# The last output chunk of five projections computed and added in two halves of 256 tokens

## The chip, the cores and the metric

The kernel runs on one core of a Trainium2 chip. The metric is the device time of one execution in microseconds (us); lower is better. Of the kernel before, three runs took 3549.62, 3550.29 and 3558.47 us, median 3550.29 us. A core has five engines that run side by side and meet at semaphores: TensorE (PE: matmuls; PEld: its weight loads), VectorE (DVE), ScalarE (ACT), GpSimd (POOL) and SyncE (SP), which issues the DMAs. Matmuls write to eight PSUM banks, each of 512 f32 columns on 128 partitions.

## The reference

A sequence of 512 tokens of width 1024 goes through two blocks. The first has two layers, each a gated feed-forward, a mixer (a recurrent hybrid in the first layer, an mLSTM in the second) and another gated feed-forward, and a final norm; the second block has attention, an RWKV mixer and a feed-forward. What the change touches are the last steps of four feed-forwards and of the mLSTM, where the output of a projection is scaled and added to the residual `x`:

```python
h = modulate(x, 0)
x = x + HALF_STEP * (1.0 + mod[:, 0, 2]) * swiglu(h, ffn_w_gate[layer, 0], ffn_w_up[layer, 0], ffn_w_down[layer, 0])
h = modulate(x, 1)
...
x = x + (1.0 + mod[:, 1, 2]) * y.astype(x.dtype)

def swiglu(h, w_gate, w_up, w_down):
    return (jax.nn.silu(h @ w_gate) * (h @ w_up)) @ w_down

def modulate(t, sub):
    return rms_norm(t, norm_g[layer, sub]) * (1.0 + mod[:, sub, 1]) + mod[:, sub, 0]
```

The mean of the squares of `x` in `rms_norm` goes over the 1024 channels of each token, so the norm behind a projection needs all of its output chunks.

## The kernel before

Activations lie with channels on the 128 partitions and the 512 tokens along the free dimension: the residual `K.x` is eight chunks (DC = 8) of 128 channels by 512 tokens. To keep f32 accuracy, weights and activations are each split into a rounded part in fp32r (`hi`) and the rest (`lo`), and each product is three matmuls: `w_hi`*`hi`, `w_hi`*`lo`, `w_lo`*`hi`.

`gemm` runs all large products. It takes the weights in tiles, four to a turn. SP loads a tile into `w_raw` (ring of four), ScalarE writes `w_hi` (`split_hi`, L253), VectorE writes `w_lo` (`split_lo`, L259), each into one of two halves of its buffer (by the tile's number, even or odd), and TensorE multiplies (L464 to L466), three matmuls for each block of 128 inputs. Behind a tile's last matmul `tile_mm` counts up. The turns run as a loop in each engine's own program, the last turn apart in straight code (`last` is true). Each engine works its program strictly in the order in which it is written; nothing but the semaphores ties them.

`project` calls `gemm` for the down projections of the four gated feed-forwards (called by `swiglu`, activations `f_gu_hi`, `f_gu_lo`, 22 input blocks) and for that of the mLSTM (`ml_hi`, `ml_lo`, 16 blocks). Two weight tiles make one output chunk (`tpo` = 2), of 11 or 8 input blocks each, accumulated in one bank: tiles j = 0, 1 of a turn in bank 0, tiles j = 2, 3 in bank 1. So a chunk is 66 matmuls of 512 columns, 48 in the mLSTM. Behind the second tile VectorE updates the residual, `x = bank * coef + x` (L1261), and counts `bank_free` up. That releases ScalarE: the square of the new chunk (L614, tiles `sq_f`, `sq_ml`; at the last feed-forward a second, scaled square, L616), then `h_hi` = `gain` * `x` (`ahead_act`, L723). GpSimd sums the squares of the first seven chunks; VectorE writes `h_lo` (`ahead_dve`, L728).

Behind each of these projections stands a gemm whose input norm is begun early (`follow`, a `Modulated`): its first tile (`early_tile`, L419 to L423) multiplies the weights with `gain` * `x` before the norm is known, chunk by chunk. Between its matmuls TensorE adds up the squares (`between`, L746) and, once VectorE has the reciprocal root, spreads it into a row (L121). The result of the early tile is scaled afterwards. The second and third tile (`next_pair`, L435, L436, banks 1 and 2) use the normed input.

Of the kernel before, what the change touches and what calls it, by code (L numbers as in the profile page):

```python
# [16 lines left out]
ALU = mybir.AluOpType  # L17
# [4 lines left out]
S = 512  # L22
NT = S // P
D = 1024
DC = D // P
FF = 2816
FC = FF // P
RING = 4
# [118 lines left out]
def setup(nc, ctx, dram):  # L147
    K = Core()
# [51 lines left out]
    K.hi_done = K.count("w_hi_done")  # L200
    K.lo_done = K.count("w_lo_done")
    K.tile_mm = K.count("tile_mm")
    K.bank_free = K.count("bank_free")

    K.ada_loaded, K.ada_base = [K.sem(f"ada_loaded{i}") for i in range(2)], 0
# [74 lines left out]
    body(n - 1, True)  # L280


def gemm(K, w, kb, n_tiles, nxt, mm, pe_wait, act_evac=None, dve_evac=None, turn=4, post=None, side=None, head=None, squares=None, fetched=RING, fetch=RING, aside=None, slots_free=None, dve_first=None, unroll=False, pe_more=None, pool_work=None, sp_more=None, dve_lead=None, ready_k=None, begun=False):

    nc = K.nc
# [5 lines left out]
    with one_block(K) as block:  # L293
# [90 lines left out]
        def _(pe):  # L384
# [3 lines left out]
            def weights(j, k):  # L388
                return K.w_hi[:, j % SPLIT, k * P:(k + 1) * P], K.w_lo[:, j % SPLIT, k * P:(k + 1) * P]

            def first_pair():
                for j in range(2):
                    pe.wait_ge(K.lo_done.sem, g0 + j + PRIMED + 1)
                    pe_wait(pe, 0, j, j)
                for k in range(kb):
                    pe.wait_ge(K.h_hi_done.sem, K.h_hi_done(k + 1))
                    for j in range(2):
                        hi, lo, bank, start, stop = mm(k, j)
                        wh, wl = weights(j, k)
                        nc.tensor.matmul(K.ps[bank][:], wh, hi, start=start, stop=False)  # L400
                        nc.tensor.matmul(K.ps[bank][:], wl, hi, start=False, stop=False)  # L401
                for j in range(2):
                    for k in range(kb):
                        hi, lo, bank, start, stop = mm(k, j)
                        pe.wait_ge(K.h_ready.sem, K.h_ready(k + 1))
                        last_mm = nc.tensor.matmul(K.ps[bank][:], weights(j, k)[0], lo, start=False, stop=stop)  # L406
                    last_mm.then_inc(K.tile_mm.sem, 1)
# [37 lines left out]
            def body(i, last):  # L445
                for j in range(turn):
                    t = turn * i + j
                    if early and isinstance(i, int) and t < 3:
                        if t == 0:
                            early_tile()  # L450
                        if t == 1:
                            next_pair()
                    elif head and isinstance(i, int) and t < 2:
                        if t == 0:
                            first_pair()
                    elif not (begun and t == 0):
                        pe.wait_ge(K.lo_done.sem, g0 + t + PRIMED + 1)
                        pe_wait(pe, i, j, t)
                        for k in range(kb):
                            if ready_k and isinstance(i, int) and t == 0:  # L460
                                ready_k(pe, k)
                            hi, lo, bank, start, stop = mm(k, j)
                            wh, wl = weights(j, k)
                            nc.tensor.matmul(K.ps[bank][:], wh, hi, start=start, stop=False)  # L464
                            nc.tensor.matmul(K.ps[bank][:], wh, lo, start=False, stop=False)  # L465
                            last_mm = nc.tensor.matmul(K.ps[bank][:], wl, hi, start=False, stop=stop)  # L466
                        last_mm.then_inc(K.tile_mm.sem, 1)
                    if pe_more:
                        pe_more(pe, t)
                    if side and last and j == turn - 1:  # L470
                        side.reduce(pe, n)
# [715 lines left out]
def swiglu(K, name, w_gu, w_down, nxt, head, gate, ada=None, double=False, follow=None):  # L1187
# [27 lines left out]
    def dve_evac(dve, i, j, t, mm_done):  # L1215
        f = 2 * i + j // 2
        if j % 2 == 1:
# [5 lines left out]
                                    gu_hi[:, bass.ds(f, 1), :].bitcast(F32), ALU.subtract).then_inc(K.gu_lo_done.sem, 1)  # L1223

    gemm(K, w_gu, DC, 2 * FC, (w_down, KB_MAX), mm, pe_wait, act_evac, dve_evac, side=side, head=head)
    low = K.gu_lo_done(0)
    for c in (done, sil_done, guhi_done, K.gu_lo_done):
# [12 lines left out]
def root_table(K, act):  # L1240

    K.nc.scalar.activation(K.pad4[:], K.consts[:, 0:NT], ACT.Sqrt)


def project(K, w, kb, tpo, mm, nxt, gate, half, squares, turn=4, side=None, ready=None, follow=None):

    nc = K.nc
    banks = turn // tpo
    free = K.bank_free

    def pe_wait(pe, i, j, t):
        if j % tpo == 0:
            pe.wait_ge(free.sem, free(banks * i + j // tpo - banks + 1))
        if ready:
            ready(pe, j)

    def dve_evac(dve, i, j, t, mm_done):
        if j % tpo == tpo - 1:
            o = banks * i + j // tpo
            dve.wait_ge(K.tile_mm.sem, mm_done)  # L1260
            nc.vector.scalar_tensor_tensor(K.x[:, bass.ds(o, 1), :], K.ps[j // tpo][:, None, :], K.coef[:, bass.ds(o, 1)], K.x[:, bass.ds(o, 1), :],  # L1261
                                           ALU.mult, ALU.add).then_inc(free.sem, 1)
            if follow:
                follow.ahead_dve(dve, o)

    def act_evac(act, i, j, t, mm_done):
        if j % tpo == tpo - 1:
            o = banks * i + j // tpo
            if isinstance(o, int) and o == DC - 1:
                root_table(K, act)  # L1270
            act.wait_ge(free.sem, free(o + 1))
            if follow:
                act.wait_ge(K.x_written.sem, K.x_written(follow.GAIN_STEPS))
            squares.by_act(act, K.x[:, bass.ds(o, 1), :], o, j // tpo % 2)
            if follow:
                follow.ahead_act(act, o)

    def coefficients(dve):
        dve.wait_ge(free.sem, free(0))
        dve.wait_ge(K.ada_out.sem, K.ada_out(0))  # L1280
        nc.vector.tensor_scalar(K.coef[:], gate, 1.0, half, ALU.add, ALU.mult).then_inc(K.coef_done.sem, 1)
        dve.wait_ge(K.coef_done.sem, K.coef_done(1))
        if follow:
            follow.gain_ahead(dve)

    gemm(K, w, kb, DC * tpo, nxt, mm, pe_wait, act_evac, dve_evac, turn=turn, side=side, squares=squares, dve_first=coefficients)
    if follow:
        follow.ahead_advance()
    free.base += DC
    K.coef_done.base += 1  # L1290
# [2427 lines left out]
def build(nc, dram, plan=None):  # L3718
    with ExitStack() as ctx:
        K = setup(nc, ctx, dram)  # L3720
        K.prod_done = K.count("prod_done")
        K.conv_step = K.count("conv_step")
# [159 lines left out]
```

## Time and profile before

| | us |
|---|---|
| median of three runs | 3550.29 |
| span of the profiled execution, first to last instruction | 3552.7 |
| time of the profiled execution around its span | not recorded apart |
| TensorE busy | 3415.0 (96%) |
| VectorE busy | 2019.4 (57%) |
| ScalarE busy | 1212.5 (34%) |
| mean granted TensorE clock | 0.982 of 2.4 GHz |

An engine that is busy for nearly all of the span sets the time wherever it has no gap. A matmul's time in the rows runs from its start to the arrival of its result, and the next starts before that; how long a stream of matmuls takes is read from the starts. The start times in the rows are us from the span's start.

### The profile page before, as it was taken

The page shows a single profiled execution, that of the slowest core. Times are in us where ns is not written, and L with a number is a line of the kernel's source. Part 1 is how long each engine was busy: PE and PEld are TensorE (multiplying, and loading weights), DVE is VectorE, ACT ScalarE, POOL GpSimd, SP SyncE. Part 2 cuts the span into 40 slices and gives each one's busy share as a digit, 9 for nine tenths or more (in the row PEclk, how much of TensorE's full clock was granted, in tenths as well). Part 3 has the DMA queues.
Part 4 walks back from the last instruction along what each step waited for, and adds up shares of the span by engine and source line. Part 5 has one row for each costly group of instructions (what it writes and reads, how often), then busy time and mean ns, then how long its engine had stood idle before and what let it go on. Part 6 is the DMA issues. An engine that isn't in the chain of part 4 may idle for free. (4 is left out here: it accounts for less than half of the span.)

```text
span 3552.7 us, 56318 instructions
## 1 busy us (share of the span) xinstructions
PE 3415.0 (96%) x22324; PEld 2767.9 (78%) x22324; DVE 2019.4 (57%) x2820; ACT 1212.5 (34%) x1783; POOL 361.9 (10%) x264
## 2 busy tenths in 40 slices
PE   7999998999999999999999999999989999999998
PEld 5888777778888788876678888877767787878886
DVE  6666666856665766574443433365666773454343
ACT  3222346432222322243243322233434543233231
POOL 1000003410000000010101000130103330010000
PEclk9999999999999999999999999999979999989999
DMA  6554322125554555421032233232210002223332
GB/s 246 194 195 174 129 74 72 56 93 189 194 204 140 183 189 205 162 87 48 1 107 94 95 97 103 90 90 82 62 37 6 7 7 68 95 66 101 95 95 77
DMA packets 103764, 382.73 MB, mean 108 GB/s; under 512 B 11424, under 2 KB 15136, under 8 KB 103200
## 3 DMA queue, kind: packets, MB, share of 16 engines
q1 hardware_dynamic: 103584, 380.15, 31.8%
q8 instruction: 135, 2.21, 0.3%
q14 instruction: 45, 0.37, 0.0%
HBM read 378.01 MB, written 2.10 MB: 107 GB/s over the span
## 5 line engine op out<-in xcount | busy, mean ns | idle before, releaser
L464 PE MATMUL bank<-h_hi,w_hi 128*128 128x512 f32 x2576 | 1015.5, 394 | 30.1 <-DVE w_lo L259 27.3
L466 PE MATMUL bank<-h_hi,w_lo 128*128 128x512 f32 x2576 | 1005.3, 390 | 0.0
L465 PE MATMUL bank<-h_lo,w_hi 128*128 128x512 f32 x2576 | 1005.1, 390 | 0.0
L259 DVE TENSOR_TENSOR w_lo<-w_raw,w_hi 128x1024 fp32r<-128x1024 f32 (+2 forms) x480 | 635.2, 1323 | 386.5 <-ACT w_hi L253 375.4
L253 ACT ACTIVATE w_hi<-w_raw 128x1024 fp32r<-128x1024 f32 (+2 forms) x475 | 521.3, 1097 | 287.7 <-PE bank L466 247.9
L464 PEld LDWEIGHTS bank<-h_hi,w_hi 128*128 128x128 f32 x2576 | 485.2, 188 | 147.2 <-DVE w_lo L259 30.7
L466 PEld LDWEIGHTS bank<-h_hi,w_lo 128*128 128x128 f32 x2576 | 485.1, 188 | 102.7
L465 PEld LDWEIGHTS bank<-h_lo,w_hi 128*128 128x128 f32 x2576 | 485.3, 188 | 100.5 <-issue 1.9
L464 PE MATMUL bank<-f_gu_hi,w_hi 128*128 128x512 f32 x704 | 274.2, 390 | 0.0
L466 PE MATMUL bank<-f_gu_hi,w_lo 128*128 128x512 f32 x704 | 273.9, 389 | 0.0
L465 PE MATMUL bank<-f_gu_lo,w_hi 128*128 128x512 f32 x704 | 273.9, 389 | 0.0
L1213 ACT ACTIVATE f_gu_hi<-f_prod_t 128x512 f32 (+1 forms) x88 | 55.6, 632 | 406.9 <-DVE f_prod_t L1220 406.9
L558 DVE SCALAR_TENSOR_TENSOR ada_acc<-ada_tiles,c_act,ada_acc 128x512 f32<-128x512 f32 x210 | 157.4, 750 | 6.9 <-DMA ada_tiles<-in_ada 1.2
L1220 DVE TENSOR_TENSOR f_prod_t<-f_sil_t,bank 128x512 f32<-128x512 f32 x88 | 60.5, 687 | 166.8 <-PE bank L466 166.8
L466 PEld LDWEIGHTS bank<-f_gu_hi,w_lo 128*128 128x128 f32 x704 | 132.1, 188 | 27.6
L464 PEld LDWEIGHTS bank<-f_gu_hi,w_hi 128*128 128x128 f32 x704 | 132.1, 188 | 27.6
L465 PEld LDWEIGHTS bank<-f_gu_lo,w_hi 128*128 128x128 f32 x704 | 132.1, 188 | 27.4
L1210 ACT ACTIVATE f_sil_t<-bank 128x512 f32<-128x512 f32 x88 | 52.7, 598 | 243.8 <-PE bank L466 243.7
L1261 DVE SCALAR_TENSOR_TENSOR residual<-bank,coef,residual 128x512 f32 (+1 forms) x40 | 30.0, 751 | 156.9 <-PE bank L466 156.9
L607 POOL MEMSET sq_acc_f<- 128x512 f32 x5 | 2.6, 528 | 1039.5 <-DVE f_gu_lo L1222 1039.5
L1222 DVE TENSOR_TENSOR f_gu_lo<-f_prod_t,f_gu_hi 128x512 f32 (+1 forms) x88 | 60.9, 692 | 77.9 <-ACT f_gu_hi L1213 77.9
L466 PE MATMUL bank<-u_hi,w_lo 128*128 128x512 f32 x256 | 99.6, 389 | 0.0
(643 smaller groups left out, 4730.2 us busy)
## 6 DMA issues: line engine op xcount, KB each, us to landing
ada_tiles<-in_ada SPq DMA_DIRECT2D x180, 512.0 KB, 4.1
w_raw<-in_gu SPq DMA_DIRECT2D x176, 512.0 KB, 4.4
w_raw<-in_dn SPq DMA_DIRECT2D x64, 704.0 KB, 4.8
w_raw<-in_w_ff SPq DMA_DIRECT2D x64, 512.0 KB, 3.6
w_raw<-in_w_hyb SPq DMA_DIRECT2D x36, 512.0 KB, 3.3
w_raw<-in_w_rkv SPq DMA_DIRECT2D x24, 512.0 KB, 3.6
w_raw<-in_w_attn SPq DMA_DIRECT2D x20, 512.0 KB, 3.6
w_raw<-in_w_hout SPq DMA_DIRECT2D x16, 512.0 KB, 3.4
```

The costliest lines, as they stand in the source:

```text
L253: K.nc.scalar.activation(K.w_hi[:, half, 0:kb * P], K.w_raw[:, slot, 0:kb * P], ACT.Copy).then_inc(K.hi_done.sem, 1)
L259: K.nc.vector.tensor_tensor(K.w_lo[:, half, 0:kb * P], K.w_raw[:, slot, 0:kb * P], K.w_hi[:, half, 0:kb * P].bitcast(F32), ALU.subtract).t ...
L464: nc.tensor.matmul(K.ps[bank][:], wh, hi, start=start, stop=False)
L465: nc.tensor.matmul(K.ps[bank][:], wh, lo, start=False, stop=False)
L466: last_mm = nc.tensor.matmul(K.ps[bank][:], wl, hi, start=False, stop=stop)
L558: ins = v.scalar_tensor_tensor(self.acc[:], block, c, self.acc[:], ALU.mult, ALU.add)
L607: self.K.nc.gpsimd.memset(acc[:], 0.0).then_inc(self.K.sq_added.sem, 1)
L1210: nc.scalar.activation(sil[:, j // 2, :], K.ps[j][:], ACT.Silu).then_inc(sil_done.sem, 1)
L1213: nc.scalar.activation(gu_hi[:, bass.ds(f, 1), :], prod[:, j // 2:j // 2 + 1, :], ACT.Copy).then_inc(guhi_done.sem, 1)
L1220: nc.vector.tensor_tensor(prod[:, j // 2, :], sil[:, j // 2, :], K.ps[j][:], ALU.mult).then_inc(done.sem, 1)
L1222: nc.vector.tensor_tensor(gu_lo[:, bass.ds(f, 1), :], prod[:, j // 2:j // 2 + 1, :], gu_hi[:, bass.ds(f, 1), :].bitcast(F32), ALU.subtract ...
L1261: nc.vector.scalar_tensor_tensor(K.x[:, bass.ds(o, 1), :], K.ps[j // tpo][:, None, :], K.coef[:, bass.ds(o, 1)], K.x[:, bass.ds(o, 1), :], ...
```

## The change

In the last turn, the last two weight tiles (j = 2 and 3, the last output chunk) are no longer multiplied with all 512 tokens at a time. `tile_in_halves` runs over the tile's input blocks for tokens 0 to 255 into columns 0 to 255 of bank 1, then again for tokens 256 to 511 into columns 256 to 511 of bank 2. Behind the last matmul of the first half of tile 3 a new semaphore, `half_mm`, counts up. VectorE updates the residual in two instructions of 256 columns: the first waits for `half_mm`, the second for `tile_mm` as before, and it alone counts `bank_free` up. ScalarE's work on the chunk, and `h_lo`, stay whole.

```diff
@@ gemm, TensorE
+            def tile_in_halves(j):
+                for part in range(2):
+                    cols = slice(part * (S // 2), (part + 1) * (S // 2))
+                    for k in range(kb):
+                        hi, lo, bank, start, stop = mm(k, j)
+                        wh, wl = weights(j, k)
+                        out = K.ps[bank + part][:, cols]
+                        nc.tensor.matmul(out, wh, hi[:, cols], start=start, stop=False)
+                        nc.tensor.matmul(out, wh, lo[:, cols], start=False, stop=False)
+                        last_mm = nc.tensor.matmul(out, wl, hi[:, cols], start=False, stop=stop)
+                    if part == 0 and j == turn - 1:
+                        last_mm.then_inc(K.half_mm.sem, 1)
+                return last_mm
...
-                        for k in range(kb):
+                        in_halves = last_in_halves and last and j >= turn - 2
+                        if in_halves:
+                            last_mm = tile_in_halves(j)
+                        for k in range(0 if in_halves else kb):
@@ project, VectorE
+    def half_evac(o, part):
+        cols = slice(part * (S // 2), (part + 1) * (S // 2))
+        x = K.x[:, o, cols]
+        return nc.vector.scalar_tensor_tensor(x, K.ps[(turn - 1) // tpo + part][:, cols], K.coef[:, o:o + 1], x, ALU.mult, ALU.add)
...
+            if isinstance(o, int) and o == DC - 1:
+                dve.wait_ge(K.half_mm.sem, K.half_mm(1))
+                half_evac(o, 0)
+                dve.wait_ge(K.tile_mm.sem, mm_done)
+                half_evac(o, 1).then_inc(free.sem, 1)
+                if follow:
+                    follow.ahead_dve(dve, o)
+                return
...
-    gemm(K, w, kb, DC * tpo, nxt, mm, pe_wait, act_evac, dve_evac, turn=turn, side=side, squares=squares, dve_first=coefficients)
+    gemm(K, w, kb, DC * tpo, nxt, mm, pe_wait, act_evac, dve_evac, turn=turn, side=side, squares=squares, dve_first=coefficients, last_in_halves=True)
+    K.half_mm.base += 1
```

TensorE's program before, where the last tile (j = 3) of the first feed-forward's down projection begins. Names: `w_hi`, `w_lo` are the split weights, `f_gu_hi`, `f_gu_lo` the split activations.

```order
L464 MATMUL bank<-f_gu_hi,w_hi 128x512
L465 MATMUL bank<-f_gu_lo,w_hi 128x512
L466 MATMUL bank<-f_gu_hi,w_lo 128x512
L464 MATMUL bank<-f_gu_hi,w_hi 128x512 [waits gu_lo_done,w_lo_done]
L465 MATMUL bank<-f_gu_lo,w_hi 128x512
L466 MATMUL bank<-f_gu_hi,w_lo 128x512
```

The same place in TensorE's program after the change.

```order
L399 MATMUL bank<-f_gu_hi,w_hi 128x256
L400 MATMUL bank<-f_gu_lo,w_hi 128x256
L401 MATMUL bank<-f_gu_hi,w_lo 128x256
L399 MATMUL bank<-f_gu_hi,w_hi 128x256 [waits gu_lo_done,w_lo_done]
L400 MATMUL bank<-f_gu_lo,w_hi 128x256
L401 MATMUL bank<-f_gu_hi,w_lo 128x256
```

The three matmuls of a block are half as wide, and from the wait to the end of the tile there are 66 of them instead of 33. The waits stay where they were; in all, TensorE's program grows by 312 matmuls in the five projections.

VectorE's program before, at the end of the same projection and the start of the next gemm. `ada_acc`, `ada_turned`, `ada_parts` and `mods` belong to modulation weights worked on in between.

```order
L259 TENSOR_TENSOR w_lo<-w_raw,w_hi 128x1024 [waits w_hi_done]
L564 STREAM_TRANSPOSE ada_turned_212<-ada_acc_211 128x512 [waits ada_step]
L566 TENSOR_REDUCE ada_parts_213<-ada_turned_212 128x16 [waits ada_turned]
L1261 SCALAR_TENSOR_TENSOR residual<-bank,coef,residual 128x512 [waits tile_mm]
L728 SCALAR_TENSOR_TENSOR h_lo<-residual,gain,h_hi 128x512 [waits h_hi_done]
L573 TENSOR_TENSOR mods<-bank,cols 128x16 [waits ada_mm]
```

The same place in VectorE's program after the change.

```order
L260 TENSOR_TENSOR w_lo<-w_raw,w_hi 128x1024 [waits w_hi_done]
L582 STREAM_TRANSPOSE ada_turned_212<-ada_acc_211 128x512 [waits ada_step]
L584 TENSOR_REDUCE ada_parts_213<-ada_turned_212 128x16 [waits ada_turned]
L1278 SCALAR_TENSOR_TENSOR residual<-bank,coef,residual 128x256 [waits half_mm]
L1278 SCALAR_TENSOR_TENSOR residual<-bank,coef,residual 128x256 [waits tile_mm]
L746 SCALAR_TENSOR_TENSOR h_lo<-residual,gain,h_hi 128x512 [waits h_hi_done]
L591 TENSOR_TENSOR mods<-bank,cols 128x16 [waits ada_mm]
```

One update became two, the first with a wait of its own; nothing else changed its place.

## Rows read from the trace of the kernel before

**Rows 1.** Page, engines' busy time; two costly groups: count, busy, mean ns, idle before.

```profile
PE 3415.0 (96%) x22324; PEld 2767.9 (78%) x22324; DVE 2019.4 (57%) x2820; ACT 1212.5 (34%) x1783; POOL 361.9 (10%) x264
...
L1220 DVE TENSOR_TENSOR f_prod_t<-f_sil_t,bank 128x512 f32<-128x512 f32 x88 | 60.5, 687 | 166.8 <-PE bank L466 166.8
...
L1261 DVE SCALAR_TENSOR_TENSOR residual<-bank,coef,residual 128x512 f32 (+1 forms) x40 | 30.0, 751 | 156.9 <-PE bank L466 156.9
```

**Rows 2.** Busy time by stretch: stretch, length, PE, PEld, DVE, ACT, POOL, clock, DMA.

```profile
393.00:408.00 15.00, 15.00 (x71) 12.15 (x69) 8.92 (x10) 5.07 (x6) 1.29 (x1) 1.00 0.11 36
...
1941.00:1952.00 11.00, 11.00 (x50) 9.09 (x49) 4.38 (x4) 4.74 (x6) 1.29 (x1) 1.00 0.16 51
```

**Rows 3.** Time order, first feed-forward's end: start us, us, instruction [idle before].

```profile
393.13 0.75 DVE L1261 SCALAR_TENSOR_TENSOR residual<-bank,coef,residual 128x512 f32<-128x512 f32 x1 [4.38 <-PE bank L466]
...
403.64 0.69 DVE L566 TENSOR_REDUCE ada_parts<-ada_turned 128x16 f32<-128x512 f32 x1
...
408.09 0.75 DVE L1261 SCALAR_TENSOR_TENSOR residual<-bank,coef,residual 128x512 f32<-128x512 f32 x1 [3.76 <-PE bank L466]
...
408.87 0.63 ACT L614 ACTIVATE sq_f<-residual 128x512 f32<-128x512 f32 x1 [5.63 <-DVE residual L1261]
...
409.41 0.71 ACT L723 ACTIVATE h_hi<-residual,gain 128x512 fp32r<-128x512 f32 x1
...
410.15 0.75 DVE L728 SCALAR_TENSOR_TENSOR h_lo<-residual,gain,h_hi 128x512 fp32r<-128x512 f32 x1 [1.31 <-ACT h_hi L723]
...
410.55 0.42 PEld L746 LDWEIGHTS bank<-consts,sq_f 128*128 128x128 f32 x2
```

**Rows 4.** Time order, the mLSTM projection's last two chunks and its end.

```profile
1941.23 0.75 DVE L1261 SCALAR_TENSOR_TENSOR residual<-bank,coef,residual 128x512 f32<-128x512 f32 x1 [3.06 <-PE bank L466]
...
1952.11 0.75 DVE L1261 SCALAR_TENSOR_TENSOR residual<-bank,coef,residual 128x512 f32<-128x512 f32 x1 [3.06 <-PE bank L466]
...
1952.90 0.63 ACT L614 ACTIVATE sq_ml<-residual 128x512 f32<-128x512 f32 x1 [3.59 <-DVE residual L1261]
...
1954.17 0.42 PEld L746 LDWEIGHTS bank<-consts,sq_ml 128*128 128x128 f32 x2
```

**Rows 5.** Time order, the early tile's first matmul on its last chunk.

```profile
416.39 0.47 PE L419 MATMUL bank<-h_hi,w_hi 128*128 128x512 f32 x1
```

**Rows 6.** Time order, the last update of the third feed-forward.

```profile
1523.93 0.75 DVE L1261 SCALAR_TENSOR_TENSOR residual<-bank,coef,residual 128x512 f32<-128x512 f32 x1 [3.76 <-PE bank L466]
```

**Rows 7.** Time order, the last feed-forward's end: second square, first read of squares.

```profile
2318.31 0.71 ACT L616 ACTIVATE sq_f<-residual,cols 128x512 f32<-128x512 f32 x1
...
2320.87 0.28 PE L746 MATMUL bank<-consts,sq_f 128*128 128x1 f32 x2
```

**Rows 8.** Weight loads of 16 and 128 columns; time order, matmuls with 16-column loads.

```profile
L1471 PEld LDWEIGHTS bank<-h_hi,w_dt_hi x8: 94/94/95, 459.9 to 464.8; 128*16 128x16 f32 x8
...
L464 PEld LDWEIGHTS bank<-f_gu_hi,w_hi 128*128 128x128 f32 x704 | 132.1, 188 | 27.6
...
460.16 0.40 PE L1471 MATMUL bank<-h_hi,w_dt_hi 128*16 128x512 f32 x1
...
465.44 0.39 PE L1471 MATMUL bank<-h_hi,w_dt_lo 128*16 128x512 f32 x1
```

**Rows 9.** Time order, mLSTM scores in f32: 512-column matmuls; loads at 256, 128.

```profile
1643.28 2.74 PE L2137 MATMUL bank<-ml_xc,ml_y 128*128 128x512 f32 x6
...
1651.04 1.70 PEld L2137 LDWEIGHTS bank<-ml_xc,ml_y 128*128 128x128 f32 x8
...
1652.77 0.86 PEld L2137 LDWEIGHTS bank<-ml_xc,ml_y 128*128 128x128 f32 x7
```

**Rows 10.** Time order, two of the early tile's matmuls, a pair of L746 between.

```profile
410.47 0.47 PE L419 MATMUL bank<-h_hi,w_hi 128*128 128x512 f32 x1
...
410.92 0.48 PE L421 MATMUL bank<-h_lo,w_hi 128*128 128x512 f32 x1
```

**Rows 11.** Groups by line and shape, a VectorE read of 256 bank columns.

```profile
L2330 DVE TENSOR_TENSOR mlh_e<-mlh_e,bank 128x256 f32<-128x256 f32 x4 | 1.7, 419 | 0.0
```

More of the change, by code:

```diff
@@ L202, in setup @@
     K.tile_mm = K.count("tile_mm")
+    K.half_mm = K.count("half_mm")
     K.bank_free = K.count("bank_free")
@@ L280, in rolled, with gemm @@
     body(n - 1, True)
-def gemm(K, w, kb, n_tiles, nxt, mm, pe_wait, act_evac=None, dve_evac=None, turn=4, post=None, side=None, head=None, squares=None, fetched=RING, fetch=RING, aside=None, slots_free=None, dve_first=None, unroll=False, pe_more=None, pool_work=None, sp_more=None, dve_lead=None, ready_k=None, begun=False):
+def gemm(K, w, kb, n_tiles, nxt, mm, pe_wait, act_evac=None, dve_evac=None, turn=4, post=None, side=None, head=None, squares=None, fetched=RING, fetch=RING, aside=None, slots_free=None, dve_first=None, unroll=False, pe_more=None, pool_work=None, sp_more=None, dve_lead=None, ready_k=None, begun=False, last_in_halves=False):
     nc = K.nc
```

## The prediction, made before the changed kernel ran

> **What bounds the kernel now.** I read the page's busy times first: TensorE is busy for 96% of the span, VectorE for 57%, and only TensorE is near to being full [rows 1]. The change touches five places, the last of eight output chunks of each of the five projections that call `project` (the four down projections of the gated feed-forwards, tile names `f_gu`, and that of the mLSTM, `ml`). So the second view is the busy time by stretch there: in the last chunks TensorE is busy for the whole stretch, at a granted clock of 1.00, that is 2.4 GHz [rows 2]. A stage without a gap on TensorE gets longer by whatever TensorE gets to do, and shorter only if the wait behind it gets shorter.
>
> The third view is the order in time around the first of these ends. A chunk of 66 matmuls of 128x512 takes 408.09 - 393.13 = 14.96 us, which is 226.7 ns per matmul [rows 3]. The mLSTM's chunk of 48 takes 1952.11 - 1941.23 = 10.88 us, again 226.7 ns [rows 4].
>
> What waits for the last residual update? It starts at 408.09 and takes 0.75 us; ScalarE then squares it (to 409.50) and writes `h_hi` (to 410.12), VectorE `h_lo` (to 410.90) [rows 3]. TensorE meanwhile has gone on with the next gemm's early tile, whose first columns read older chunks. It first needs the last square for the sum of squares, whose weight load starts at 410.55 [rows 3]: 1.05 us after the square was there. It needs `h_lo` of the last chunk only at 416.39 [rows 5], and the root, the row and the scaled input hang on TensorE's own sums. The two ends after it, of which one row stands [rows 6], repeat this pattern. At the mLSTM the square ends at 1953.53 and its load starts at 1954.17, 0.64 us later [rows 4]; at the last feed-forward the second square ends at 2319.02 and is read at 2320.87 [rows 7]. So at none of the five ends does TensorE wait for the update.
>
> **The change part by part.**
>
> TensorE's work. The last two weight tiles of each projection go from 33 (mLSTM: 24) matmuls of 512 columns each to twice as many of 256, each with its own weight load. That is 4 x 66 + 48 = 312 matmuls replaced by 624, in both tiles, not only in the one whose end is waited for. They take 312 x 0.2267 = 70.7 us now. The new time is 624 x p, where p is the spacing of 256-column matmuls of this type with a 128x128 load each. The trace has none in fp32r, so I bound it:
>
> - From below by the load alone. A load of 16 columns takes 94 ns and one of 128 takes 188 [rows 8], so 0.839 ns a column, 107.4 ns for 128 columns. 624 x 0.1074 - 70.7 = -3.7 us.
> - The mLSTM's scores in plain f32 show the same situation: their 128-column records stream for as long as 256 columns do here (two clocks a column, since the 256-column ones come every (1.70 - 0.19)/7 = 0.216 us) and carry a full load, and they come every (0.86 - 0.19)/6 = 0.112 us [rows 9]. So loads of 188 ns are started every 112 ns, and load and stream overlap. p = 0.112: 69.9 - 70.7 = -0.8 us.
> - If the excess over pure streaming is a share of the columns, p = 226.7/2 = 113.4 ns and the change costs nothing.
> - If the excess is fixed per matmul: 512 columns at 2.4 GHz are 213.3 ns, so it is 13.4 ns; p = 106.7 + 13.4 = 120.1 ns, and the cost is 312 x 13.4 ns = 4.2 us.
> - If the load's spacing and the excess add: the early tile gives (0.45 - 0.227)/2 = 0.112 us for each of the two full loads with one column behind it that lie between two of its matmuls [rows 3, 10]; p = 112 + 13.4 = 125.4 ns, +7.5 us.
> - Farthest: a load must be over (188 ns) before the next matmul starts. 624 x 0.188 - 70.7 = +46.6 us.
>
> I take the fixed excess, 120 ns. Two rows speak for it. The spacing stays at (465.44 - 460.16)/23 = 0.230 us where the load has 16 columns instead of 128 [rows 8], so the excess isn't load time left uncovered. And in f32 the excess does not grow with the columns: (2.74 - 0.59)/5 = 0.43 us apart at 512 columns (426.7 ns of streaming, 3 over), 0.216 at 256 (213.3, again 2 to 3 over) [rows 9]. Result: +3.5 us at the feed-forwards, 264 x 13.4 ns, and +0.6 at the mLSTM, 48 x 13.4 ns.
>
> Here a page of the Trainium skill speaks against the change. "Perfetto Trace Analysis", section "Matmuls", says that larger matmuls are more efficient than smaller ones; "TensorE: Matmul & The Clock Gate", section "Back-to-back issue gap", puts a warm matmul at its columns over 2.4 GHz plus about 2.5 ns, that is 215.8 and 109.2 ns. By it, as an estimate, the change would cost 312 x 2.5 ns = 0.8 us. The trace has 226.7 ns for 512 columns of fp32r, so of its excess the page has a fifth, and the measurement decides.
>
> VectorE's work. One update of 751 ns from a bank becomes two of 256 columns. Reads of a bank with two operands take 687 ns at 512 columns [rows 1] and 419 at 256 [rows 11], 1.05 ns a column, so a half takes 751 - 268 = about 0.48 us. The first half's matmuls end some 33 x 0.12 = 4.0 us before the second's; its 0.48 us lies in the time in which VectorE waits anyway (3.76 us idle ahead of the update) [rows 3]. Only the second half is left behind the last matmul, and the update ends 0.27 us earlier. It is worth nothing, since TensorE needs what follows 0.64 us later than it has it, or more. Behind the new wait for `half_mm` stand on VectorE only the second half, `h_lo`, and `w_lo` of the next gemm; no one needs the latter two earlier than before. If both halves fell behind the last matmul, the update would end 2 x 0.48 - 0.75 = 0.21 us later, and that is covered too.
>
> ScalarE, GpSimd, SP. Their order doesn't change. They see the last two tiles end about 0.44 and 0.88 us later, while the next gemm's first tile is split into `w_hi` and `w_lo` and stored in a part of the buffer that the last tile doesn't read; that is done well inside the last tile's 7.9 us. No DMA is added. Bank 2, which now takes the second half, is next written by the pair of tiles behind the early tile, which come after the matmul at 416.39 [rows 5], 7 us behind the update. The new matmuls stand in straight code, so 312 more pairs of load and matmul are fetched; I cost that at nothing, since the f32 pairs of rows 9 came every 112 ns. If that cover were gone it would be a case of rival 1.
>
> **Sum.** +4.2 us of TensorE, 0 on the rest. The profiled execution's span is 3552.7 us, 2.4 us over the median of the runs, 3550.3, whose own scatter is 3549.6 to 3558.5. On the median: 3550.3 + 4.2 = 3554.5 us, or +0.12%. About 0.3%, 10.7 us, is what a measurement of this kernel can tell from no change, so this reads as the same.
>
> **Rivals.**
>
> 1. The load shows (slower). With half the columns to hide under, the fp32r load and its switch into the array aren't covered. For it: load and stream are now equally long, 107 ns each, where before the stream had twice the load's length; no row shows this pair in fp32r. Against it: f32 with the same two lengths comes at 112 ns [rows 9]. It decides from p = (70.7 + 10.7)/624 = 130.5 ns; at 125 ns the kernel still reads the same. At 188 ns: 3550.3 + 46.6 = 3596.9 us; at 140, 3566.9 us.
> 2. Smaller pieces cost nothing, and the earlier update counts (slightly faster, but within the 0.3%). p = 112 ns gives -0.8 us; if all five ends passed on the 0.27 us, -1.4 more: 3548.1 us. Against it: the slack of 0.64 us or more at each end. A gain of over 0.3% has no row: even p at the load's floor with all updates counted gives -5.1 us, 3545.2.
> 3. The change doesn't do what it says: the first half's update runs together with the second's, since VectorE is late or the semaphore comes late. VectorE's last piece of work ahead of it ends at 404.33 [rows 3], about when the first half is ready (408.09 - 4.0 = 404.1). It costs 0 as worked out, so the time is that of the forecast, 3554.5; only the trace would tell.
>
> **How the numbers follow.** Forecast (fixed excess, +1 to +8 us), with rival 3 in it: 0.70. Excess by share or less, rival 2: 0.15. Rival 1 beyond 130.5 ns: 0.12. A gain of over 0.3% by a mechanism that I don't see: 0.03. So faster 0.03, same 0.85, slower 0.12. The likeliest one's own range is 3551.3 to 3558.3. The range goes from rival 2 with a microsecond of scatter, 3547, to above the sum of load spacing and excess (3557.8) with the runs' scatter, 3561; about 0.08 of rival 1 is left out above, some 0.05 below.
>
> **What would show it.** In the groups by line the matmuls of 256 columns should be 1.1 to 1.25 us per ten apart, and each last chunk of a feed-forward 15.8 us long instead of 14.96, the mLSTM's 11.5 instead of 10.88. The first half's update should stand about 4 us before the second's, each near 0.48 us, and the square should start 0.27 us sooner after the last matmul, with TensorE's next wait unchanged. I am wrong if the last chunks are 14.9 us or shorter (then the excess goes by columns, rival 2), if they are over 17.2 us (rival 1), or if TensorE's sum of squares moves up against the end of the projection.

## The result and the profile after

Slower, by more than was forecast. Five runs of the changed kernel took 3561.44 to 3571.29 us, median 3565.12, beside 3551.0 us for the kernel before on the same chip: ratio 1.0038, 95% interval 1.0024 to 1.0052. The forecast was 3554.5 us and its range ended at 3561. So some 4 us were foreseen and some 9 to 10 were not. The profiled run is the slowest of the five; its page begins:

```profile
span 3569.5 us, 56947 instructions
...
PE 3426.7 (96%) x22636; PEld 2789.8 (78%) x22636; DVE 2021.1 (57%) x2825; ACT 1212.8 (34%) x1783; POOL 359.6 (10%) x264
```

TensorE has 22636 - 22324 = 312 matmuls more [rows 1] and the same share of a longer span. The stretches of the two kinds of last chunk, columns as in [rows 2]:

```profile
393.00:409.00 16.00, 16.00 (x139) 15.79 (x138) 9.48 (x12) 5.13 (x7) 1.29 (x1) 1.00 0.11 34
1942.00:1954.00 12.00, 12.00 (x95) 11.65 (x94) 4.87 (x5) 4.75 (x6) 1.29 (x1) 1.00 0.25 89
```

TensorE is still without a gap there, at 2.4 GHz, and its weight loads now fill 15.79 of 16 us where they filled 12.15 of 15 [rows 2]. The matmuls themselves in time order (start us, us, engine, line, operation):

```profile
394.54 0.28 PE L399 MATMUL bank<-f_gu_hi,w_hi 128*128 128x256 f32 x1
394.66 0.28 PE L400 MATMUL bank<-f_gu_lo,w_hi 128*128 128x256 f32 x1
394.78 0.28 PE L401 MATMUL bank<-f_gu_hi,w_lo 128*128 128x256 f32 x1
```

They start 0.12 us apart. The end of the first feed-forward, which answers to [rows 3], idle time before each in brackets:

```profile
392.59 0.75 DVE L1292 SCALAR_TENSOR_TENSOR residual<-bank,coef,residual 128x512 f32<-128x512 f32 x1 [4.38 <-PE bank L484]
...
404.46 0.48 DVE L1278 SCALAR_TENSOR_TENSOR residual<-bank,coef,residual 128x256 f32<-128x256 f32 x1 [0.24 <-PE bank L401]
...
408.42 0.48 DVE L1278 SCALAR_TENSOR_TENSOR residual<-bank,coef,residual 128x256 f32<-128x256 f32 x1 [3.47 <-PE bank L401]
408.94 0.63 ACT L632 ACTIVATE sq_f<-residual 128x512 f32<-128x512 f32 x1 [5.80 <-DVE residual L1278]
...
410.89 0.42 PEld L764 LDWEIGHTS bank<-consts,sq_f 128*128 128x128 f32 x2
```

The last chunk takes 408.42 - 392.59 = 15.83 us, 0.87 more than before. The first half is updated 3.96 us ahead of the second, and the square starts 0.52 us after the last update's start instead of 0.78 [rows 3]: 0.26 us earlier. TensorE loads that square at 410.89, 1.32 us after it was there. The mLSTM's end, which answers to [rows 4]:

```profile
1944.10 0.75 DVE L1292 SCALAR_TENSOR_TENSOR residual<-bank,coef,residual 128x512 f32<-128x512 f32 x1 [3.06 <-PE bank L484]
...
1955.61 0.48 DVE L1278 SCALAR_TENSOR_TENSOR residual<-bank,coef,residual 128x256 f32<-128x256 f32 x1 [2.40 <-PE bank L401]
```

11.51 us instead of 10.88. So all five places cost 4 x 0.87 + 0.63 = 4.1 us, as forecast. The rest is not at the places that were edited: at the last of them the last update starts 4.3 us later than before (2321.31 instead of 2316.99), at the start of the RWKV stage, which the change doesn't touch, the trace is 6 us behind, at that stage's end 11 and at the kernel's end 17. By stretch, the kernel before:

```profile
2695.00:2958.00 263.00, 245.34 (x7300) 211.23 (x7299) 182.04 (x399) 123.42 (x230) 89.93 (x59) 1.00 0.03 7
2958.00:2989.00 31.00, 25.02 (x169) 17.32 (x159) 15.09 (x24) 11.77 (x16) 0.00 (x0) 0.94 0.26 87
```

The changed one:

```profile
2701.00:2969.00 268.00, 246.81 (x7271) 211.85 (x7263) 182.17 (x399) 123.50 (x230) 89.39 (x59) 0.99 0.03 7
2969.00:3006.00 37.00, 29.05 (x184) 20.04 (x184) 15.09 (x24) 11.66 (x16) 0.00 (x0) 0.86 0.25 86
```

The same work has 268.0 - 246.8 = 21.2 us without a matmul instead of 17.7, and a stretch at 1.2 GHz follows behind it (granted clock 0.86 instead of 0.94 over a stretch 6 us longer).

### The profile page after: what moved, and what is told of

It reads as the page before. It is cut to its first block and busy times, and to the rows that moved or that the text cites. A ratio compares the mean times of both kernels' runs of the same rounds, so it can differ in the third digit from the quotient of the medians.

```text
span 3569.5 us, 56947 instructions
## 1 busy us (share of the span) xinstructions
PE 3426.7 (96%) x22636; PEld 2789.8 (78%) x22636; DVE 2021.1 (57%) x2825; ACT 1212.8 (34%) x1783; POOL 359.6 (10%) x264
## 5 line engine op out<-in xcount | busy, mean ns | idle before, releaser
L482 PE MATMUL bank<-f_gu_hi,w_hi 128*128 128x512 f32 x616 | 240.0, 390 | 0.0
L484 PE MATMUL bank<-f_gu_hi,w_lo 128*128 128x512 f32 x616 | 239.7, 389 | 0.0
L483 PE MATMUL bank<-f_gu_lo,w_hi 128*128 128x512 f32 x616 | 239.6, 389 | 0.0
L482 PEld LDWEIGHTS bank<-f_gu_hi,w_hi 128*128 128x128 f32 x616 | 115.6, 188 | 24.3
L484 PEld LDWEIGHTS bank<-f_gu_hi,w_lo 128*128 128x128 f32 x616 | 115.6, 188 | 24.0
L483 PEld LDWEIGHTS bank<-f_gu_lo,w_hi 128*128 128x128 f32 x616 | 115.7, 188 | 23.9
L482 PE MATMUL bank<-u_hi,w_hi 128*128 128x512 f32 x256 | 99.6, 389 | 0.0
```

## Where TensorE runs out of instructions

What ended the idle time ahead of TensorE's weight loads in that stage (us, times, longest), the kernel before:

```profile
PEld bank L3200 <- issue: 8.1, 19, 0.8
...
PEld bank L3320 <- issue: 2.4, 2, 1.3
```

The changed one; L3232 and L3352 are the same lines of the program:

```profile
PEld bank L3232 <- issue: 11.2, 23, 1.1
...
PEld bank L3352 <- issue: 2.1, 1, 2.1
```

"issue" means that nothing in the profile released the engine. The transfers show what some of it was. In the transfers of 8 us of the changed kernel (GB/s in 40 slices of 0.2 us) the only ones are of instructions:

```profile
GB/s 0 0 82 0 0 0 0 0 0 0 0 0 0 0 0 0 0 0 0 0 0 0 82 0 0 0 0 0 0 0 0 0 0 0 0 0 0 0 0 0
...
q8 instruction: 2, 0.03, 1.5%
```

They start at 2930.4 and 2934.5 us. TensorE's loads after a pause, same time:

```profile
2932.91 0.13 PEld L3333 LDWEIGHTS bank<-rw_rbkT,rw_W 64*64 64x64 f32 x1 [0.77 <-issue]
2936.94 0.13 PEld L3352 LDWEIGHTS bank<-rw_b_tok,rw_W 64*64 64x64 f32 x1 [2.07 <-issue]
```

Each instruction packet of this queue in the trace has 16384 bytes. The stage's 57 packets (this view, both kernels) stand against some 14,600 loads and matmuls (7300 and 7299 in the row of the kernel before above), which makes 256 instructions a packet. I counted TensorE's instructions through the trace: both of these pauses end at the same place modulo 256 (number 90 of the records), exactly 256 records apart, 1.4 and 1.6 us after a packet has landed. I take that place for the first instruction of a block. A pause is measured here from the start of the instruction before it, so it is some 0.1 us longer than the idle time in the rows. Taking all pauses of over 0.35 us at such a block start that end 1.2 to 1.7 us after a landing, the kernel before has 10, of 10.3 us together, all in the RWKV stage; the changed one 16, of 16.5 us. The other "issue" pauses of that length in the stage stand elsewhere in the blocks, and there are some 20 of them in either trace: those at block starts are what has grown, from 10 to 16. There the code is straight and pairs of load and matmul follow each other within some 20 ns where nothing is waited for, so a block is used up in 2 to 3 us, while the closest transfers of these traces start 3.3 us apart. Where a block holds a wait for VectorE or GpSimd, the next one arrives meanwhile. Where a whole block falls into fast code, TensorE pauses at both its ends, as at 2932.91 and 2936.94. In the kernel before the block starts fall elsewhere in the same code:

```profile
2925.28 0.13 PEld L3312 LDWEIGHTS bank<-rw_W,rw_b_tok 64*64 64x64 f32 x1 [0.89 <-issue]
2927.19 0.54 PEld L3200 LDWEIGHTS bank<-rw_abT_T,rw_off 64*64 64x64 f32 x16 [0.17 <-POOL rw_off L3103]
```

One pause of 0.89 us, none at L3320, and at 2927.19 TensorE waits for GpSimd as it should. In the changed kernel it comes late there instead.

The Trainium skill, "Runtime: NRT & Kernel Launch", section "Instruction fetch mechanics", describes this: instructions arrive in blocks of 16 KiB, 256 of them, the next one fetched while the present one runs. On the size the trace agrees. The page also holds that crossing a block is mostly hidden, and names taken branches as what makes an engine wait for its instructions; here code without a branch pauses 10 to 16 us. The experiments are to tell whether the pauses make the loss.

## The experiments

Each ratio stands against runs of the kernel before on the same chip; e13 ran once and has none. Each kernel's time is split in two parts: the mean over its runs of span x granted clock, and the rest, span x (1 - clock). The first is roughly the time if the clock had never fallen to 1.2 GHz, the second what the fallen clock took. A mean over 8 to 12 runs is good to about 1 us in either part, one over 5 to about 2. The kernel before has 3483.7 + 67.0 us over 99 runs on four chips, whose means at full clock agree within 0.4 us; the two columns are differences from it. "Pauses" are those at block starts, from one profile of each.

| kernel | median us | ratio and interval | at full clock | lost to clock | pauses, us |
|---|---|---|---|---|---|
| before | 3551 to 3553 | | 0 | 0 | 10, 10.3 |
| changed (both series, 10 runs) | 3565.12, 3567.04 | 1.0038 (1.0024 to 1.0052), 1.0037 (1.0024 to 1.0050) | +9.4 | +4.0 | 16, 16.5; 17, 16.1 |
| e1 more matmuls | 3555.99 | 1.001 (1.0001 to 1.0019) | +4.1 | -0.4 | 10, 8.5 |
| e2 624 waits | 3558.75 | 1.0016 (1.0007 to 1.0025) | +4.9 | +1.2 | 16, 14.6 |
| e3 changed + 656 waits | 3565.46 | 1.0029 (1.0019 to 1.0039) | +10.1 | +1.2 | 11, 10.4 |
| e4 changed + 400 waits | 3556.15 | 1.0013 (1.0004 to 1.0022) | +4.7 | +0.3 | 11, 9.5 |
| e5 changed, one update | 3565.6 | 1.0035 (1.0022 to 1.0049) | +9.3 | +2.9 | 17, 14.2 |
| e6 38 waits | 3552.6 | 0.9996 (0.9987 to 1.0005) | -0.3 | -0.5 | 14, 9.4 |
| e7 1024 waits | 3554.44 | 1.0 (0.9991 to 1.001) | 0.0 | +0.8 | 10, 9.0 |
| e8 112 waits | 3564.57 | 1.0027 (1.0018 to 1.0037) | +6.0 | +3.9 | 16, 14.1 |
| e9 192 waits | 3559.71 | 1.002 (1.0011 to 1.0028) | +5.6 | +1.5 | 14, 13.7 |
| e10 64 waits | 3552.53 | 1.0 (0.9991 to 1.0009) | +1.3 | -1.4 | 14, 10.2 |
| e11 112 waits, all at the last place | 3557.62 | 1.0015 (1.0005 to 1.0024) | +5.3 | -0.4 | 19, 16.9 |
| e12 changed + 144 waits | 3557.86 | 1.0017 (1.0008 to 1.0026) | +4.7 | +0.3 | 11, 10.7 |

**The changed kernel again**, unaltered.

> The changed kernel once more, unaltered. The first measurement gave +14 us (3565.1 against 3551.0), of which its trace shows only 4.3 us in the five last chunks (matmuls 120 ns apart as forecast, 0.93 us per feed-forward and 0.6 at the mLSTM); the rest lies elsewhere, most of it in the RWKV stage and beside stretches at the lower clock. Theory A (the rest is systematic and comes from TensorE's program being 624 instructions longer, which moves the code behind it): again +14 us, 3565. Theory B (the rest is chance of that set of runs, the lower-clock stretches falling differently): +4.3 us, 3555. Theory C (the rest is systematic and comes from the delay itself, which moves the later stages in time): again +14 us.

It repeats: 3567.04 us (3562.07 to 3568.26). Not chance.

**The matmuls' cost alone (e1), and the length of the code alone (e2).** e1 adds to the kernel before as much matmul time as the halves, 19 matmuls of 512 columns into the unused bank 2, hence 38 instructions:

```diff
+                            if extra and last and j >= turn - 2 and k == kb - 1:
+                                for _ in range(extra[j - turn + 2]):
+                                    nc.tensor.matmul(K.ps[2][:], wh, hi, start=True, stop=True)
```

> The kernel before, with the last chunk whole, but with 19 more matmuls of 512 columns into bank 2 (2 in each of the last two tiles of the four feed-forwards, 1 and 2 in those of the mLSTM): 19 x 0.2267 = 4.3 us more of TensorE at the same five places, and only 38 more instructions in its program. The results in bank 2 are not read. Theory A (code length): +4.3 us and little more, 3555. Theory B (chance): +4.3 us, 3555. Theory C (the delay has consequences): +14 us, 3565.

e2 adds as many instructions as the halves, 624, but waits that are satisfied already, up to two ahead of a matmul. Two calls of `wait_ge` in a row become one instruction, hence the `2 * n`: TensorE has 1161 semaphore instructions in e2's trace and 537 in that of the kernel before.

```diff
+            def fill(wanted):
+                n = min(pad[0], left[0]) if wanted else 0
+                left[0] -= n
+                for _ in range(2 * n):
+                    pe.wait_ge(K.lo_done.sem, g0 + PRIMED)
...
+                            fill(pad and last and j >= turn - 2)
                             nc.tensor.matmul(K.ps[bank][:], wh, hi, start=start, stop=False)
```

> The kernel before, with the last chunk whole, but with two more semaphore instructions (waits that are long satisfied) ahead of each matmul of the last two tiles, 624 in all: TensorE's program is as much longer as in the changed kernel, at the same five places, with no work added to the array. The waits should be hidden while the matmuls are 226.7 ns apart. Theory A (code length): about +10 us, 3561. Theory B (chance) and theory C (delay): 0, 3551. If the waits aren't hidden, the last chunks get longer, and their length in the trace says by how much.

e1 costs 4.1 us at full clock and moves nothing else: a delay of this size is passed on once and starts nothing. e2 does no work and costs 4.9 us at full clock (its expectation had about 10 us in all by the length of the code; 6.1 were found in the mean span). Its matmuls still come every 0.22 to 0.23 us:

```profile
1943.78 0.39 PE L473 MATMUL bank<-ml_hi,w_hi 128*128 128x512 f32 x1
1944.00 0.39 PE L475 MATMUL bank<-ml_lo,w_hi 128*128 128x512 f32 x1
1944.23 0.39 PE L477 MATMUL bank<-ml_hi,w_lo 128*128 128x512 f32 x1
```

So its loss isn't where the waits are. The place of the code behind them is left.

**The changed kernel with its code moved on to a multiple of 256 (e3, e4, e12).** The waits of e2 in the first two tiles of the last turn (`j < turn - 2`): e3 fills up each of the five places to 256 instructions, e4 leaves out the mLSTM and reaches 1024 in all, e12 reaches 768.

> The changed kernel, with satisfied waits between the 512-column matmuls of the two tiles ahead of the halves (124 per feed-forward, 160 in the mLSTM), so that each of the five places adds 256 instructions to TensorE's program instead of 132 or 96. If the rest of the loss is the position of the later code relative to blocks of a power of two up to 256 instructions (theory A in its narrow form), it goes: +4.3 us, 3555. If it is the mere amount of code (A in its wide form), it doubles or so: +14 to +25 us. Theory B: +4.3 us. Theory C: +14 us.

> The changed kernel, with satisfied waits between 512-column matmuls ahead of the halves, at most two per matmul (in e3 four per matmul set the spacing at 0.44 us in the mLSTM's projection and cost some 7 us; two were hidden): 124 in each of the first three feed-forwards, 28 in the last, none in the mLSTM. TensorE's program is 1024 instructions longer than before the change when the RWKV stage begins, 4 x 256. Theory A (the position of the later code relative to blocks of 256 instructions; pauses of TensorE without a releaser stand at instructions 89 to 92 modulo 256 in all traces so far): the RWKV stage from 2695 to 2957 us is as long as before the change, within 0.5 us, and the kernel costs +4.3 us for the matmuls and up to 2 for the stretch at 549 us: 3556 to 3558. Theory A' (amount of code): +14 us or more, 3566.

> The changed kernel with 36 satisfied waits in the first two tiles of the last turn of each of the four feed-forwards, 144 in all: with the 624 instructions that the halves add this is 768, three blocks of 256. Place theory: only the cost of the matmuls is left, +4.3 us over the kernel before (+3 to +7), and the RWKV stage has 10 to 11 pauses at block starts of 9 to 10.5 us together. Rival (the recovery with 1024 had to do with where those waits stood or with chance): +11 to +14 us as in the changed kernel, and about 16 pauses of 14 to 16.5 us.

e3 gave nothing back in all, for a reason of its own: four waits ahead of each of the mLSTM's matmuls are too many.

```profile
1943.84 0.47 PE L491 MATMUL bank<-ml_hi,w_hi 128*128 128x512 f32 x1
1944.28 0.47 PE L493 MATMUL bank<-ml_lo,w_hi 128*128 128x512 f32 x1
1944.72 0.47 PE L495 MATMUL bank<-ml_hi,w_lo 128*128 128x512 f32 x1
```

At 0.44 us each they made that stage 6 to 7 us longer, which hid the recovery; the pauses were back at 11, of 10.4 us. e4 and e12, without that, both fall to 4.7 us over the kernel before at full clock, which is the matmuls' cost, and lose nothing to the clock. In e4 the RWKV stage answers to the kernel before (262.0 - 244.7 = 17.3 us without a matmul, 17.7 there):

```profile
2697.00:2959.00 262.00, 244.74 (x7250) 210.56 (x7243) 181.62 (x399) 123.49 (x230) 89.97 (x59) 1.00 0.03 7
2959.00:2991.00 32.00, 26.04 (x211) 18.32 (x203) 15.44 (x26) 11.78 (x16) 0.00 (x0) 0.95 0.26 88
```

and its idle time ahead of the same line is again what it was, to the tenth:

```profile
PEld bank L3243 <- issue: 8.1, 19, 0.8
```

More instructions made the changed kernel 8.3 us faster in the mean span (3564.0 to 3555.7). The waits replaced nothing, so what they did was to move the later code. The stretch at the lower clock near 549 us, of which the expectations of e4 and e5 speak, isn't a mark of the halves: between 545 and 556 us the granted clock is 1.00 in e4 and e12, which hold them, and 0.84 in e9, which doesn't.

**One update again (e5).** The matmuls stay in halves, both into bank 1, `half_mm` goes, and VectorE updates all 512 tokens behind the last:

```diff
-                        out = K.ps[bank + part][:, cols]
+                        out = K.ps[bank][:, cols]
...
-            if isinstance(o, int) and o == DC - 1:
+            if False:
```

> The changed kernel with the halves of the matmuls kept, but both into bank 1, without the semaphore for the first half, and with the residual updated whole in one instruction behind the last matmul. If the early half of the update is worth nothing (the forecast): the same time as the changed kernel, 3566, within 2 us. If it is worth the 0.27 us at each of the five ends: 1.4 us more, 3567. If part of the loss (the extra stretch at the lower clock near 549 us, seen in three of three traces with halves and in none of the others) comes from VectorE's two updates: 1 to 3 us less, 3563.

3565.6 us, as with two updates. The earlier update gains nothing that can be measured.

**Moving the code of the kernel before (e6 to e11).** The waits of e2, of other numbers: 38, 1024, 112 (624 less twice 256), 192 and 64, spread over the feed-forwards, and in e11 all 112 at the last of the places.

> The kernel before, with 38 satisfied waits in the last two tiles of the five projections (8 in each feed-forward, 6 in the mLSTM) and no other work: the later code of TensorE stands where it stands in e1. There the RWKV stage from 2695 to 2957 us was 2.9 us shorter than before the change. Theory A: the same here, -2 to -3 us in that stage, 3549 to 3551 in all. Theory A' (amount of code) and chance: 0 in that stage, within 0.5 us.

> The kernel before, with 256 satisfied waits in the last turn of each of the four feed-forward projections (two per matmul), 1024 in all, and no other work. Theory A: the later code keeps its place relative to blocks of 256, so the RWKV stage is as long as before within 0.5 us and the time is 3552 within 1.5 us. Theory A' (amount of code): 1024 instructions cost more than the 624 of e2, which cost 5.7 us: +9 us, 3561.

> The kernel before, with 112 satisfied waits (28 in each feed-forward projection) and no other work. 112 is what 624, the lengthening by the change, leaves over 512. Theory A (place relative to blocks of 256 instructions): the RWKV stage from 2695 to 2957 us is as long as with the change and in e2, 266 to 268 us instead of 262.4, and the time is +4 to +6 us, 3557 to 3559. Theory A'' (any lengthening that isn't a multiple costs in proportion to its amount): 112/624 of e2's loss, +1 us, 3554, and 263.4 us in the stage.

> The kernel before, with 192 satisfied waits (48 in each feed-forward projection). A scan for the place of the later code at which the pauses cost least. Theory A says only that the stage's length will lie in the band seen so far, 259 to 268 us, and be set by the place; theory A'' says +1.8 us in the stage, 264.2.

> The kernel before, with 64 satisfied waits (16 in each feed-forward projection). As e9: at 38 the stage took 259.4 and 260.9 us, at 112 it should take 266 to 268, so theory A says 260 to 268 here; theory A'' says +0.6 us, 263.0.

> The kernel before with 112 satisfied waits of TensorE (no array work), all in the last two tiles of the fourth feed-forward, the last of the five places ahead of the RWKV stage; nothing ahead of 2300 us moves. Place theory (what counts is where the RWKV stage's code stands against blocks of 256 instructions): the same loss as with four times 28 waits, which was 9.6 us; at least its part at full clock, about 6 us, so +5 to +10 us on the median, with about 16 pauses at block starts of 14 us together in the RWKV stage, where the kernel before has 10 of 10.3 us. Rival (the loss came from the moved code of the stages ahead, or from the waits themselves): 0 to +3 us, and 10 pauses of 9 to 10.5 us.

1024 instructions without work cost 0.9 us in the mean span, 112 cost 9.8, 192 cost 7.2; 38 and 64 change it by less than 1 us. That order can't come from what the waits take. Nor is it a matter of blocks of 128: 192 and 64 leave the same over 128, and cost 5.6 and 1.3 us at full clock. Two forecasts of size missed. e8 was to cost 4 to 6 us and cost 9.8, of which 3.9 went to the clock. e6 was to gain 2 to 3 us, since the RWKV stage had been that much shorter in e1's profile; the stage was 1.5 us shorter in e6's, but the kernel gained 0.3 us at full clock, within the noise. In e8, the same instruction as in the changed kernel has the same pause:

```profile
2927.46 0.13 PEld L3312 LDWEIGHTS bank<-rw_rbkT,rw_W 64*64 64x64 f32 x1 [1.06 <-issue]
2931.48 0.13 PEld L3331 LDWEIGHTS bank<-rw_b_tok,rw_W 64*64 64x64 f32 x1 [2.06 <-issue]
```

e11, which moves nothing ahead of 2300 us, keeps all of e8's loss at full clock (5.3 and 6.0 us) and has the long pause too, but none of its loss to the clock (-0.4 and +3.9, each good to 1.5):

```profile
PEld bank L3211 <- issue: 11.6, 21, 1.4
...
PEld bank L3331 <- issue: 2.1, 1, 2.1
```

So moving what follows 2320 us is enough for the loss at full clock, and the extra pauses, which all lie in the RWKV stage, go with it: kernels whose pauses sum to 8.5 to 10.7 us lose nothing beyond their own work (e10's +1.3 us at most), those with 13.7 to 16.9 us lose 4.9 to 6.0. The sum of the pauses rises by 3.4 to 6.6 us in these; the two numbers agree for the group, not kernel by kernel. The stage itself, from its first matmul on `rw_rbkT` or `rw_TT` to its last, is 286.7 us at full clock in the profile of the kernel before, 288.0 to 290.7 in the seven with 13.7 us of pauses or more (two of them are the changed kernel's) and 284.0 to 286.8 in the seven others. So the two groups don't overlap, but only 1.3 to 4.0 us of the loss are found in the stage itself; where the rest lies is not shown.

**A stream made to run out (e13).** 768 tiny matmuls in a row, 1536 instructions that wait for nothing:

```diff
+                                for m in range(stream):
+                                    r = slice(64 * (m % 2), 64 * (m % 2) + 64)
+                                    nc.tensor.matmul(K.ps[2 + m % 2][0:64, 0:16], wh[r, 0:64], hi[r, 0:16], start=True, stop=True)
```

> The kernel before with 768 tiny extra matmuls (64x64 load, 16 columns, alternating between two row groups and banks 2 and 3) ahead of the last block of the fourth feed-forward's last tile: 1536 instructions, six blocks of 256, that do nothing for the result and wait for nothing. Fetch theory (a block of 256 instructions can't follow the one before in less than the 3.3 to 3.5 us that stand between the closest instruction transfers of the RWKV stage): if a pair takes under 26 ns, TensorE pauses at each block start, each pause ends 1.2 to 1.7 us after an instruction transfer has landed, and the six blocks take 6 x 3.4 = 20 us or more. Rival (the instructions are always there in time): no pause at the block starts, the stream takes 768 times the spacing of a pair. If a pair takes over 27 ns by itself, the stream tells nothing on it.

It doesn't tell whether the fetch sets a pace. The stream took 37.6 us, 49 ns a pair, over the 27 ns from which it could have told, and there is no pause in it. The granted clock was half, 1.2 GHz, for most of the stretch:

```profile
2318.00:2360.00 42.00, 42.00 (x768) 41.27 (x764) 1.37 (x2) 2.51 (x4) 0.00 (x0) 0.55 0.01 2
```

One thing it does show: six instruction transfers start within the 37.6 us in which the 1536 instructions run, so a transfer is indeed 256 of TensorE's instructions.

## Why the prediction was wrong

- **Matmuls in halves: right.** Spacing 0.120 us as taken, last chunks 15.83 and 11.51 us where 15.8 and 11.5 were forecast. The fixed excess of 13.4 ns per matmul held against the share of the columns and against f32's 112 ns. The 2.5 ns of the Trainium skill's page ("TensorE: Matmul & The Clock Gate", section "Back-to-back issue gap"), which that section states for a matmul by itself and not, as the prediction took it, for a stream of them, were off by a factor of five here at 256 columns too. e4 and e12, where the code stands at a multiple of 256 again, show +4.7 us at full clock for the forecast's +4.2.
- **Two updates: right.** 484 ns each (0.48 forecast), 3.96 us apart (4.0), the square 0.26 us sooner (0.27), TensorE with slack at each end, and e5 the same time with one update. Rival 2 and rival 3 fell with it.
- **Rival 1** had the sign, slower, but its mechanism, a weight load that shows, didn't occur: its mark was p = 130.5 ns, and 120 was found.
- **The failed step: "The new matmuls stand in straight code, so 312 more pairs of load and matmul are fetched; I cost that at nothing."** At the place where I looked it does cost nothing. What it left out is that 624 more instructions move everything behind them against the blocks of 256, and that there is a stage behind them whose speed hangs on that. The reason given there, f32 pairs every 112 ns, fits only slow code: at that pace a block of 128 pairs lasts 14 us, in the RWKV stage 2 to 3. Nor is it a case of rival 1, as the prediction says, since the halves' own spacing stayed at 120 ns. 624 is 112 modulo 256. e11 puts the term at +5.3 us for 112 added right ahead of that stage, e2, which moves all as the halves do, at +4.9.
- **The low clock.** The changed kernel lost 4.0 us more to 1.2 GHz than the kernel before, +-1.4. e4, e12 and e1 did not; e8 did (3.9) and e5 probably (2.9), e11 did not. Two of the kernels that lose it hold the halves and one holds no work at all, so it doesn't need the halves; whether it goes with the moved code of the stages ahead, and where it arises, stays open. In the changed kernel's profile it shows right behind the RWKV stage (0.86 above), between 2330 and 2342 us (0.86, before 1.00) and between 2890 and 2910 (0.91, before 1.00), in e8's also between 1657 and 1728 us (0.88, before 0.91).

The account: 4.2 us for the matmuls, 5.3 for the moved code (e11), 4.0 for the clock, in all 13.5; the mean span grew by 3564.0 - 3550.7 = 13.3 us. The first two have a cause that the experiments show; the third is a measured difference whose cause is open. No kernel was faster than the kernel before by more than the noise. The halves cost 4 to 5 us for nothing even where their code is moved back.

## What to carry to other kernels

Count the instructions that a change adds to an engine's straight code, not only their time: code far behind it moves against the blocks in which it is fetched, and a stage of short instructions behind it can gain or lose more than the edit itself. Before an effect of a few tenths of a per cent is put down to an edit, pad it up to a multiple of 256 instructions with waits that are satisfied, no more than two per matmul of 512 columns; what remains is the edit's. And don't cut up matmuls for the sake of an earlier consumer without a row in which that consumer is late: half the columns cost 13.4 ns each here, and nothing was waiting.

## What was not expected of the hardware

- TensorE can run out of instructions in straight code without any branch: 10 to 19 pauses of 0.4 to 2.2 us at block starts, each ended 1.2 to 1.7 us after a 16384-byte instruction packet landed.
- A pair of satisfied waits per matmul is free behind a matmul of 512 columns (0.227 us apart with two wait instructions); with four the matmuls come every 0.44 us, 111 ns per wait instruction if the waits alone set that pace.
- 112 instructions that do nothing cost more than 1024 of them: 9.8 us against 0.9 in the mean span.
- A stream of 16-column matmuls that kept TensorE busy without a gap (42.00 of 42 us, its loads 41.27) ran at half clock for most of its length (granted 0.55).
